# State-space decays from bf16 row parts instead of f32 running sums

## The reference, cut to what matters

```python
def segsum_exp(a):
    cs = jnp.cumsum(a, axis=-1)
    diff = cs[..., :, None] - cs[..., None, :]
    mask = jnp.tril(jnp.ones((t, t), dtype=bool))
    return jnp.where(mask, jnp.exp(jnp.where(mask, diff, 0.0)), 0.0)

# in ssd_chunked: da = dt * a, cs = cumsum(da) within a chunk
    scores = cb[:, :, :, None] * segsum_exp(da)
    y_diag = einsum("bcgrqs,bcsgrp->bcqgrp", scores, xdt)
    decay_from_start = jnp.exp(cs)
    y_off = einsum("bcqgn,bcgrpn,bcgrq->bcqgrp", cc, states_in, decay_from_start)
```

## Time and profile before

| | |
|---|---|
| median of 3 runs | 1421.48 us (1421.24 to 1424.57) |
| profiled execution, its own time | 1420.15 us |
| its span (first to last instruction) | 1418.1 us |
| granted clock of TensorE, mean | 0.993 of 2.4 GHz |
| busy: TensorE, VectorE, ScalarE, GpSimd | 1367.4, 1044.8, 890.8, 335.1 us |
| state-space region | about 690 to 985 us |

### The profile page before, as it was taken

The page is one execution under the profiler, slowest core; times in us unless marked ns, Lnnn a source line. Parts: engine busy times, 40 slices in busy tenths (PEclk is TensorE's granted clock), DMA queues, the critical chain, the costliest instruction groups (busy, mean ns, idle before and its releaser), DMA issues.

```text
span 1418.1 us, 29905 instructions
## 1 busy us (share of the span) xinstructions
PE 1367.4 (96%) x11462; PEld 1260.7 (89%) x11462; DVE 1044.8 (74%) x1570; ACT 890.8 (63%) x1689; POOL 335.1 (24%) x326
## 2 busy tenths in 40 slices
PE   6998999999999999999899999999999999999998
PEld 6997999998888999999888989888788899899998
DVE  6797855567577865568999999867797686666554
ACT  5555744457577554467887878848667565655543
POOL 2000410115001210032855535410411031411110
PEclk9999999999999999999999999999999999999999
DMA  8332565554843555554444444434455454356551
GB/s 321 135 120 90 180 207 182 203 183 146 195 135 118 195 193 195 191 179 161 166 149 150 149 157 142 155 114 138 158 176 176 138 198 149 114 184 199 187 202 66
DMA packets 35608, 233.80 MB, mean 165 GB/s; under 512 B 4000, under 2 KB 7072, under 8 KB 8352
## 3 DMA queue, kind: packets, MB, share of 16 engines
q1 hardware_dynamic: 31104, 223.75, 45.9%
q10 hardware_dynamic: 3216, 4.19, 1.9%
q0 software_dynamic: 1168, 4.20, 1.0%
HBM read 227.93 MB, written 4.19 MB: 164 GB/s over the span
## 4 chain that ended last, share of the span: by engine, by line
PE 75%; DVE 16%; ACT 4%; issue 3%; DMA 0%; DVEq 0%; ACTq 0%; SPq 0%
PE ps L469 12%; PE ps L470 11%; PE ps L479 11%; PE ps L538 7%; PE ps L539 6%; PE ps L544 6%; DVE w_lo L1926 5%; DVE arena L2346 2%; PE ps L880 2%; PE ps L881 2%; PE ps L884 2%; DVE xa_both L1941 2%; PE ps L521 2%; PE ps L522 1%; PE ps L524 1%
## 5 line engine op out<-in xcount | busy, mean ns | idle before, releaser
L1926 DVE TENSOR_TENSOR w_lo<-raw,w_hi 128x1024 bf16<-128x1024 f32 x420 | 548.3, 1308 | 202.1 <-ACT w_hi L1199 201.8
L1199 ACT CAST w_hi<-raw 128x1024 fp32r<-128x1024 f32 x420 | 438.5, 1047 | 304.0 <-PE ps L544 133.8
L469 PE MATMUL ps<-xa_both,w_hi 128*128 128x256 f32 x1296 | 326.3, 293 | 12.0 <-ACT w_hi L1199 10.3
L470 PE MATMUL ps<-xa_both,w_hi 128*128 128x256 f32 x1296 | 309.1, 280 | 0.0
L469 PEld LDWEIGHTS ps<-xa_both,w_hi 128*128 128x128 f32 x1296 | 247.2, 191 | 18.3 <-issue 12.0
L470 PEld LDWEIGHTS ps<-xa_both,w_hi 128*128 128x128 f32 x1296 | 247.7, 191 | 0.5
L538 PE MATMUL ps<-xb_both,w_hi 128*128 128x256 f32 x832 | 204.7, 289 | 0.0
L539 PE MATMUL ps<-xb_both,w_hi 128*128 128x256 f32 x832 | 195.2, 277 | 0.0
L479 PE MATMUL ps<-xa_bf,w_lo 128*128 128x256 bf16 x1296 | 169.4, 274 | 1.2 <-DVE w_lo L1926 1.1
L2705 POOL TENSOR_TENSOR arena<-arena 128x256 f32<-128x256 f32 x96 | 69.7, 727 | 388.7 <-DVE arena L2008 388.7
L538 PEld LDWEIGHTS ps<-xb_both,w_hi 128*128 128x128 f32 x832 | 156.6, 188 | 1.6 <-DVE xb_both L1941 0.2
(11 more groups left out here) (350 smaller groups left out, 2368.2 us busy)
## 6 DMA issues: line engine op xcount, KB each, us to landing
raw<-weights SPq DMA_DIRECT2D x210, 1024.0 KB, 4.9
band<-arena ACTq DMA_DIRECT2D x1, 3072.0 KB, 35.6
arena<-band POOLq DMA_DIRECT2D x8, 256.0 KB, 3.2
arena<-gla_masks SPq DMA_DIRECT2D x1, 1088.0 KB, 15.2
H<-x_t SPq DMA_DIRECT2D x2, 512.0 KB, 4.6
arena<-band POOLq DMA_DIRECT2D x8, 128.0 KB, 2.7
arena<-mem_t POOLq DMA_DIRECT2D x1, 1024.0 KB, 5.9
out_t<-H ACTq DMA_DIRECT2D x8, 128.0 KB, 2.0
```

Of the source, the lines that this page charges most:

```text
L469: mm(ps[:, bank, 0:T], w_hi[:, s, k], X.hi[:, k], start=k == 0, stop=False)
L470: mm(ps[:, bank, 0:T], w_hi[:, s, k], X.lo[:, k], start=False, stop=False)
L1199: nc.scalar.copy(w_hi[:, j % HI_SLOTS].rearrange("p k n -> p (k n)"), raw[:, j // 2 % RING, j % 2]).then_inc(hi_done, 1)
L1926: TT(w_lo[:, j % HI_SLOTS].rearrange("p k n -> p (k n)"), raw[:, j // 2 % RING, j % 2], w_hi[:, j % HI_SLOTS].rearrange("p k n -> p (k n)" ...
```

## The change

The running sums of all heads are computed once, heads on the partitions, three times over on partitions 0 to 95. ScalarE rounds them to bf16; VectorE takes the rest and ScalarE rounds it again, and once more, so that `row_parts` (96 x 256, bf16) holds a high, a middle and a low part of each head's row. `row_pick` (96 x 32, bf16) is three identities of 32. A product of a head's column of `row_pick`, repeated, with `row_parts` adds the three parts of that head on all partitions. `ssd_quad` and `ssd_y` use it in place of the f32 products. The hand-over goes ScalarE (step 4), VectorE (5), ScalarE (6), VectorE (7). The scratch for GpSimd's DMAs is halved.

```diff
+        row_parts = sb("row_parts", [ROWS, T], BF16)          # ROWS = 3 * SSD_HEADS = 96
+        row_pick = sb("row_pick", [ROWS, SSD_HEADS], BF16)
...
+        def row_sums():
+            return ps[0:ROWS, 4, :].rearrange("p (a b) -> p a b", a=4)[:, 0:4:3]
...  TensorE, running_sums
+                for t in range(NT):
+                    for i in range(3):
+                        mm(row_sums()[i * SSD_HEADS:(i + 1) * SSD_HEADS, t], da_m[:, t * SSD_HEADS:(t + 1) * SSD_HEADS], upto_m,
+                           start=True, stop=True)
...  ssd_turn, t == 0 and g == 0 (ssd_quad, q == t == 0, gets the same wait beside its own)
-                    pe.wait_ge(sa["bias"], 1)
+                    pe.wait_ge(sa["row3"], 1)
...  ssd_quad
-                    h = t * SSD_HEADS + 8 * g + 4 * q + i
-                    mm(ps[:, 5, i * P:(i + 1) * P], da_m[:, h:h + 1].to_broadcast([P, P]), upto_m, start=i == 0, stop=False)
+                    h = 8 * g + 4 * q + i
+                    mm(ps[:, 5, i * P:(i + 1) * P], row_pick[:, h:h + 1].to_broadcast([ROWS, P]), row_parts[:, t * P:(t + 1) * P],
+                       start=i == 0, stop=False)
...  ssd_y
-                            col = da_m[:, SSD_HEADS + h + i:SSD_HEADS + h + i + 1].to_broadcast([P, 64])
-                            last = mm(ps[64 * i:64 * i + 64, 2, T + ch * P:T + (ch + 1) * P], col, upto_m, start=True, stop=True)
+                            last = mm(ps[64 * i:64 * i + 64, 2, T + ch * P:T + (ch + 1) * P], row_pick[:, h + i:h + i + 1].to_broadcast([ROWS, 64]),
+                                      row_parts[:, P:T], start=True, stop=True)
...  ScalarE, at the start of the kernel
+            for i in range(3):
+                rows = slice(i * SSD_HEADS, (i + 1) * SSD_HEADS)
+                ins = nc.scalar.copy(row_pick[rows], con[rows, CCOL["ident"] + i * SSD_HEADS:CCOL["ident"] + (i + 1) * SSD_HEADS])
+            ins.then_inc(bf_set, 1)
...  ScalarE, lead-in, behind the cast of the step
+                    if s == 4:
+                        act.wait_ge(sa["bias"], 1)
+                        nc.scalar.copy(row_parts.rearrange("p (t l) -> p t l", t=NT), row_sums()).then_inc(sa["row1"], 1)
+                    if s == 6:
+                        act.wait_ge(sa["rest1"], 1)
+                        for part in (slice(SSD_HEADS, 2 * SSD_HEADS), slice(2 * SSD_HEADS, ROWS)):
+                            ins = nc.scalar.copy(row_parts[part], row_rest[part])
+                        ins.then_inc(sa["row2"], 1)
...  VectorE, lead-in, behind the split of the step
+                if s == 5:
+                    dve.wait_ge(sa["row1"], 1)
+                    TT(row_rest.rearrange("p (t l) -> p t l", t=NT), row_sums(), row_parts.rearrange("p (t l) -> p t l", t=NT),
+                       ALU.subtract).then_inc(sa["rest1"], 1)
+                if s == 7:
+                    dve.wait_ge(sa["row2"], 1)
+                    late = slice(2 * SSD_HEADS, ROWS)
+                    TT(row_parts[late], row_rest[late], row_parts[late], ALU.subtract).then_inc(sa["row3"], 1)
...  kernel()
-    nc = bacc.Bacc("TRN2", target_bir_lowering=False, num_devices=1, dynamic_dma_scratch_size=8192)
+    nc = bacc.Bacc("TRN2", target_bir_lowering=False, num_devices=1, dynamic_dma_scratch_size=4096)
```

More of the change, by code:

```diff
@@ L88 @@
 DIFF_OUT += [[(k, n) for p in pairs for k in (6, 7) for n in (2 * p, 2 * p + 1)] for pairs in ((0, 1), (2, 3))]
+ROWS = 3 * SSD_HEADS
 HN_K, HN_Q = 2 * DIFF_HEADS, 2 * DIFF_HEADS + 2
@@ L301, in program @@
         s_off = cut(2, P)
+        row_rest = Cut(cut.at)(T, rows=ROWS)
         s_sq = cut(2, T)
@@ L351, in program @@
         sa = {n: sem("s_" + n) for n in ("tap", "silu", "z", "dtf", "dts", "dt", "dtx", "dta", "dte", "da", "cs", "bias", "x", "xd", "cb", "cbs", "c", "e",
-                                         "sc", "y", "yd", "sq", "n", "r", "on", "eb", "nx", "gb")}
+                                         "sc", "y", "yd", "sq", "n", "r", "on", "eb", "nx", "gb", "row1", "rest1", "row2", "row3")}
         merged_done = sem("merged_done")
@@ L789, in _ @@
                 v_or_q(i)
-            pe.wait_ge(bf_set, 2)
+            pe.wait_ge(bf_set, 3)
             pe.wait_ge(band_set, 1)
```

## The result

| kernel | median, us | lowest to highest | ratio to before, 95% interval |
|---|---|---|---|
| before (20 runs) | 1422.1 | 1420.46 to 1424.57 | |
| after (20 runs) | 1425.32 | 1421.71 to 1428.74 | 1.002 (1.0012 to 1.0028) |

The change costs about 3 us. The forecast was 1417.7 us, the range ended at 1422.5: both are missed, to the slow side. The profiled execution of after took 1427.29 us (span 1425.4), near the upper end of its runs and 7.1 us above the profiled one of before; so its rows show where time goes, and more of it than the median run loses; 2.7 of the 7.1 us arise at 1011 us, far behind the change.

What follows compares the result with a forecast made beforehand. VectorE was taken to bound the state-space part up to 892 us, TensorE's chain afterwards. Terms of -0.8, -3.57 and +0.55 gave -3.8 us, hence a median of 1417.7 us; range 1413.5 to 1422.5.

Steps and rivals of the forecast that it cites:

- a faster TensorE gains there only what VectorE idles: State-space part up to 892 us: VectorE's own sequence sets the pace; its idle time was 0.3 us at 794, 1.5 at 849 to 859.
- What VectorE and ScalarE get more: Lead-in near 713 to 718 us: two subtractions cost VectorE 0.7 us (0.4 to 2); ScalarE's copies and waits cost nothing.
- The quads: 16 quads on TensorE: four bf16 products replace four f32 ones, saving 0.65 us each, with 0.45 kept for the range.
- The decays of the second half: Eight y places on TensorE: two pairs of products become bf16, saving 0.27 us a pair, 0.54 a place.
- What TensorE gets more: Second chunk, about 692 us: six f32 products of 128 columns add 1.3 us, covered by TensorE's waits for VectorE.
- The new waits: TensorE's waits for row3 at step 11; row3 is ready at step 7, some 5 us earlier.
- The scratch: Smaller scratch for GpSimd's DMAs touches 17 single transfers; costed at nothing, or twice a 2.7 us wait on the attention's chain.
- The sum from 892 us on: TensorE's chain behind 892 us: three places and three quads save 3.57 us, less 0.55 for waiting on GpSimd's last convolution sum.
- most of the gain is swallowed: Rival, chance 0.18: savings of 892 to 950 us become TensorE's wait for ScalarE, full from 950.3 to 968; 1419.5 to 1420.8 us.
- Collisions: Rival, chance 0.09: from 690 to 762 us, eight more VectorE splits meet GpSimd sums at 1.1 us each; 1426.5 us.
- The rival of the other sign: Rival, chance 0.18: three fewer VectorE splits meet GpSimd's sums; 1414.4 us.
- TensorE was the bound after all: Rival, chance 0.03: TensorE bounds the state-space part, so the whole 14.7 us is gained; 1406.8 us.

Runs made afterwards that it cites:

- e8: Changed kernel with the hand-over spread over later steps, f32 products kept in groups 0 to 2, bf16 ones in group 3 only: 1419.95 us, ratio 0.9981.
- e9: Changed kernel with spread hand-over and unread filler products on TensorE before the third y, 10 in group 1, 20 in group 2: 1416.69 us, ratio 0.9962.
- e5: Changed kernel with only the hand-over spread out: ScalarE's copies at steps 5 and 8, VectorE's second subtraction at 9: 1421.79 us, ratio 0.9998.
- e2: Changed kernel with the f32 products put back in quads and y; row parts made and handed over but not read: 1425.29 us, ratio 1.0034.
- e3: Changed kernel with one rounding for all three row parts, without subtractions and further copies; bf16 products stay: 1421.41 us, ratio 1.0002.
- e7: Kernel before without the quads' decay products, plus 12 unread filler products on TensorE ahead of the third y of groups 1 and 2: 1417.33 us, ratio 0.9956.
- e4: Kernel before with the quads' f32 decay products left out, 14.2 us less TensorE work, and nothing added: 1420.17 us, ratio 0.9992.
- e6: Changed kernel with spread hand-over and 12 unread filler products on TensorE ahead of the third y of groups 1 and 2: 1417.49 us, ratio 0.9964.
- e1: Changed kernel with unread filler products on TensorE: 12 before the third y of groups 0 to 2, 8 before the first C-B scores: 1420.87 us, ratio 1.0001.

## Why the prediction was wrong

**The step that failed** is the one under the whole argument, that up to 892 us "a faster TensorE gains there only what VectorE idles". It took TensorE's extra waiting as free. The forecast itself said "TensorE's waits for L2407 longer by about 1 us in each group"; it is most of the saving of a group that falls into that one wait. From (1,11) to (2,10) after saves 3.3 us (+4.7 to +1.4), four quads and two y places, and the wait of the third y of group 2 is 2.9 longer, 4.74 against 1.85. In group 1 it is 2.5 longer, 4.09 against 1.58, with another 0.95 in the new wait at 811 us. And TensorE comes out of it at 1.2 GHz, into products that it has to do in time. No term and no rival of the prediction held the granted clock, though the column was in the earlier trace rows with 1.00 in each row. In before no fall followed the waits of 1.58 and 1.85 us; behind those of 4.09 and 4.74 in after the clock was at half for 3.4 and 6.8 us. The Trainium skill (TensorE: Matmul & The Clock Gate, Part 1: The HAM clock gate) says that the gate's setting follows how busy the engine has been recently, with 1.2 GHz for an idle one. The traces agree in the direction: each fall between 690 and 985 us, in all runs, lies at a wait of TensorE of 2.06 us or more. They don't make it a matter of the wait's length alone: of the 22 waits that long in this stretch, two, both of 2.15 us (e8 at 966.9, e9 at 961.1), had no fall.

The other half of the same step failed as well: VectorE's sequence is not fixed. Where nothing disturbed the lead-in, cheaper products on TensorE let VectorE release the third y's of groups 1 and 2 up to 4.3 us earlier (e5: 823.08 against 827.41 us, 889.02 against 892.31), where the forecast had them 0.4 later and 0.8 earlier. Why is told under the collisions.

**What VectorE and ScalarE get more** was the second miss: 0.7 us, with 2 as the worst, and ScalarE "at nothing" with 1 us left for the range. It measured 2.6 to 2.7 us in the trace up to group 3 and 4.1 in the median (e2), what the half clock behind the wait took included. The durations were right where nothing collided (0.41 us for the first subtraction; 0.42 for the second in e5, but 1.38 in after, where GpSimd's sum of 720.17 to 722.24 us runs beside it). What was wrong is the lag: the prediction had seen that the subtraction comes not before 714 us and let ScalarE wait for it with a full queue of casts, SiLUs and convolution products behind. It expected the lag to be given back by 723 us; instead TensorE stood 3.0 us at 725 and paid with the half clock. e5 and e8 show that the same instructions cost nothing three steps apart.

**The quads**: 0.66 us each, forecast 0.65. Right: four in a run take 0.23 us to the next product's start (0.89 in before), so neither 0.45 nor 0.57 was needed. **The decays of the second half**: 0.32 to 0.39 us a place, forecast 0.54; a pair goes from 0.37 to 0.18. **What TensorE gets more**: the six f32 row sums take 0.57 us (693.00 to 693.57), not 1.3; they are only 32 wide. **The new waits** on row3: none was seen. **The scratch**: nothing to be seen up to 690 us beyond 0.8 us either way, as much as the experiments scatter there.

**The sum from 892 us on** was -3.57 with 0.55 taken back for GpSimd. e8, which makes only group 3 cheaper, has much of that: 3.4 us by the rows, 0.5 back at GpSimd, about 0.5 at ScalarE, -2.4 at the end. So "most of the gain is swallowed" had its mechanism at 968 us, but of the size of 0.5.

**Collisions.** They did not make it slower: from 690 to 762 us the splits took 36.69 us for 21 before, 35.57 for 21 in after. The rival of the other sign was real where no wait disturbed the lead-in: the 21 splits from 690 us to the third y of group 0 take 36.05 us in before and 33.15 in e5, 2.9 less, and VectorE released that y at 760.08 instead of 762.79 us. That is why VectorE, thought to be immovable, moved in e3 to e7, by 0.4 to 4.3 us at the third y's of groups 1 and 2. That GpSimd's work is what lengthens a split shows in the timelines. In before, 23 of the 64 splits from 690 to 914 us have no GpSimd instruction beside them, and none of these takes over 1.23 us; the other 41 take 1.73 on average and up to 2.35. In e5 it is 20 with at most 1.23, and 45 with 1.62 on average. No experiment moved GpSimd's sums alone.

**TensorE was the bound after all** got a chance of 0.03; e4, with 14.2 us less to do and -1 us in the time, bears out that it was low.

**What stays open:** how the median's 3.2 us divide between the two causes. The parts don't just add: hand-over alone +4.1, products with a hand-over that costs nothing (e5) 0, both +3.2. The falls between 964 and 974 us and the one near 1005 us, which before has too, follow waits for ScalarE's square (2.15 us at 963.9 in e6; 4.04 at 1011.5 in after, with 6.8 us at half clock), and no experiment was made on them. In e8 and e9 the clock stays full at the first of these places, behind a wait as long, and why is open too. Whether the later profiled 2.7 us at 1011 belong to the change at all isn't shown.

## What to carry to other kernels

Where two engines are both nearly full, list the waits of the faster one before making it faster still: what is saved ahead of such a wait doesn't vanish, it is added to the wait, and on TensorE a longer wait can be paid a second time, in the products behind it: so it was here at 20 of 22 waits of 2.06 us or more. Compare the granted clock stretch by stretch, and either save only where TensorE is the last to arrive (e8), or keep it at work through the wait (e6). A chain that passes a small tile to and fro between two engines with full queues wants its links several steps apart; where it is put is worth more than what it computes.

## What the runs showed of the hardware

- A wait of TensorE of 2.06 to 2.22 us was followed by 3.4 us at 1.2 GHz in all five places of the table, one of 4.09 or 4.10 by 3.4 us (two places), one of 4.74 to 4.81 by 6.8 us (four); none of 1.85 or less by any. Elsewhere in the same runs the length of a wait does not tell it: 2.15 us at L579 was followed by no fall in e8 and e9 and by 3.4 us in e1, e5 and e6; 3.00 us at 725 by 6.8 in after, 3.02 by 3.4 in e2; 4.04 at 1011 by 6.8 in after, 4.06 by 3.4 in e3. A length of a fall follows from a window's mean: in e6 the 5 us from 889 to 894 stand at 0.66, so 3.4 of them at half clock. These are this kernel's places, and no rule is drawn from them for others.
- From a y to the end of its chunk, 3.4 us at the full clock became 6.2 us (e5), 4.9 us with the shorter fall (e6: 888.72 to 893.66).
- Twelve bf16 products of 512 columns, 0.22 us apart, kept the clock up in group 1 of e6 and e7, where they filled the wait, and not in group 2, where 2.14 and 2.22 us were left; what they cost was what they overran the wait by, about half a microsecond in e6's group 1.
- Four bf16 products of 128 columns on 96 partitions, each with its own weights, go 0.06 us apart, as the pair in the earlier trace rows did.
- VectorE's 128 x 1024 subtraction of two SBUF operands took at most 1.23 us with no GpSimd instruction beside it, and up to 2.35 with one (before, 64 of them).
